# Gate, up and down of an expert: six transfers of 1 MB become three of 2 MB

## What is computed

```python
def one_block(args):
    tok, e, w = args
    xb = xt[tok]
    hb = jax.nn.silu(xb @ w_gate[e]) * (xb @ w_up[e])
    return (hb @ w_down[e]) * w[:, None].astype(h.dtype)
```

## Time and profile before

| | us |
|---|---|
| median of 3 runs | 1754.09 |
| lowest and highest | 1751.27, 1755.17 |
| the profiled execution | 1756.78 |
| its span, first to last instruction | 1754.9 |
| PE busy with matmuls | 1347.4 (77%) |
| DVE, ACT, POOL busy | 439.7, 177.8, 206.6 |
| moved by the transfer engines | 400.32 MB, 228 GB/s over the span |

### The profile page before, as it was taken

One profiled execution on the slowest core, in us unless ns is written; L12 is line 12 of the kernel. 1 busy time (PEld: TensorE's weight loads), 2 busy tenths in 40 slices (PEclk: granted clock), 3 DMA queues, 4 the chain that ended last, 5 costly groups with the idle time before them and its releaser, 6 DMA issues.

```text
span 1754.9 us, 27286 instructions
## 1 busy us (share of the span) xinstructions
PE 1347.4 (77%) x10122; PEld 690.7 (39%) x10123; DVE 439.7 (25%) x966; ACT 177.8 (10%) x464; POOL 206.6 (12%) x364
## 2 busy tenths in 40 slices
PE   7959987689667887787669999879437688887740
PEld 1124444432334444454312444655234344544420
DVE  0021126737301111111036001552640011111106
ACT  0000023300000000000001001441000000000000
POOL 0000000000011222222110000000001112222120
PEclk9979996789688898888779999598657778989875
DMA  9942330037199799899997542001029999598940
GB/s 344 357 152 96 115 101 1 1 119 252 51 395 396 287 385 401 330 377 400 404 365 235 130 125 87 22 1 48 24 74 398 406 406 391 196 399 314 361 140 36
DMA packets 102356, 400.32 MB, mean 228 GB/s; under 512 B 13765, under 2 KB 14053, under 8 KB 80809
## 3 DMA queue, kind: packets, MB, share of 16 engines
q1 hardware_dynamic: 79544, 341.88, 51.3%
q0 software_dynamic: 16848, 55.23, 9.4%
q10 hardware_dynamic: 5924, 2.71, 0.6%
HBM read 383.18 MB, written 16.74 MB: 228 GB/s over the span
## 4 chain that ended last, share of the span: by engine, by line
PE 46%; DMA 34%; DVE 8%; issue 4%; ACT 4%; DVEq 1%; POOL 1%; SPq 0%; POOLq 0%; ACTq 0%
DMA ring<-in_w_up_dram 20%; PE ps L694 19%; DMA xg<-xmod,idx 10%; PE ps L657 5%; PE ps L878 4%; PE ps L672 4%; PE ps L896 3%; PE ps L862 2%; PE ps L784 2%; ACT hT L575 2%; DMA mbias<-in_b_ada_dram 2%; PE ps L817 1%; DVE sums L1071 1%; DMA qkv<-ybuf 1%; PE ps L769 1%
## 5 line engine op out<-in xcount | busy, mean ns | idle before, releaser
L878 PE MATMUL ps<-ring,xs 128*32 128x256 f32 x4736 | 310.2, 417 | 91.6 <-DMA ring<-in_w_up_dram 78.7
L878 PEld LDWEIGHTS ps<-ring,xs 128*32 128x32 f32 x4736 | 172.2, 119 | 225.4 <-issue 143.1
L694 PE MATMUL ps<-ring,hT 128*128 128x512 f32 x576 | 250.3, 596 | 4.5 <-ACT hT L539 2.3
L896 PE MATMUL ps<-ring,hm 128*32 128x256 f32 x2368 | 190.2, 475 | 1.4 <-DMA ring<-in_w_down_dram 1.4
L694 PEld LDWEIGHTS ps<-ring,hT 128*128 128x128 f32 x576 | 109.8, 191 | 143.6 <-issue 136.9
L862 PE MATMUL ps<-cst,xg 32*128 32x32 f32 x608 | 93.5, 277 | 81.1 <-DMA xg<-xmod,idx 81.1
L862 PEld LDWEIGHTS ps<-cst,xg 32*128 32x128 f32 x608 | 77.5, 195 | 129.0 <-issue 121.7
L1300 DVE TENSOR_TENSOR hp<-sg,ps 128x128 f32<-128x128 f32 x74 | 21.3, 288 | 371.6 <-ACT sg L622 371.6
L896 PEld LDWEIGHTS ps<-ring,hm 128*32 128x32 f32 x2368 | 82.5, 132 | 68.4 <-issue 38.8
L672 PE MATMUL ps<-ring,cond 128*2 128x512 f32 x192 | 91.4, 633 | 4.1 <-issue 4.1
L657 PE MATMUL ps<-ring,cond 128*2 128x512 f32 x192 | 84.3, 602 | 10.3 <-ACT cond L520 10.3
(11 more groups left out here) (197 smaller groups left out, 964.9 us busy)
## 6 DMA issues: line engine op xcount, KB each, us to landing
ring<-in_w_gate_dram SPq DMA_DIRECT2D x82, 1024.0 KB, 14.7
ring<-in_w_up_dram SPq DMA_DIRECT2D x82, 1024.0 KB
ring<-in_w_down_dram SPq DMA_DIRECT2D x82, 1024.0 KB, 15.9
ring<-in_w_ada_dram SPq DMA_DIRECT2D x48, 1024.0 KB, 10.6
ring<-in_w_qkv_a_dram SPq DMA_DIRECT2D x12, 1024.0 KB, 4.9
ring<-in_w_qkv_b_dram SPq DMA_DIRECT2D x12, 1024.0 KB, 7.4
modb<-mdram POOLq DMA_DIRECT2D x16, 512.0 KB, 7.9
qkv<-ybuf POOLq DMA_DIRECT2D x2, 3072.0 KB, 18.8
```

The source lines that it names most:

```text
L694: ins = mm(ps[:, 2 * t + hf, :], lhs[:, k, t * P:(t + 1) * P], raw[:, slot, kk * D + hf * 512:kk * D + (hf + 1) * 512], start=(k == 0), st ...
L878: ins = mm(ps[j * BLK:(j + 1) * BLK, 1, 0:W].rearrange("p (a n) -> p a n", a=2), xs[:, k, :], w[:, :, at:at + FW], start=(k == 0), stop=(k ...
L896: ins = mm(ps[j * BLK:(j + 1) * BLK, 5, 0:WD], hm[:, 2 * c + q, :], ring[:, slot + GU + c, q * D + j * WD:q * D + (j + 1) * WD], start=(c ...
```

## The change

Each of the three matrices of an expert comes in one transfer of 2 MB. Gate now lies in slots 0 and 1, up in slots 2 and 3, down in slots 4 and 5; the halves k = 0 to 3 and 4 to 7 of a matrix are its two slots. `taken` names the second half of a block for every slot. `gate_up` waits once, for both matrices, and `down` once.

```diff
         def taken(l, s, start):
 
-            return (gu_used[l], start * 2 + (s // 2 + 1)) if s < GU else (dn_used[l], start * 2 + (s - GU + 1))
+            return (gu_used[l], start * 2 + 2) if s < GU else (dn_used[l], start * 2 + 2)
...
-                    for s in range(RING):
+                    for s in range(0, RING, 2):
                         if isinstance(i, int):
-                            sp.wait_ge(st_free, MOE0[l] + s + 1)
+                            sp.wait_ge(st_free, MOE0[l] + s + 2)
                         else:
 
                             sp.wait_ge(*taken(l, s, freed))
 
                             sp.wait_ge(moe_land[l][s], i * 16 + 16)
-                        dst = ring[:, bass.ds(base + s, 1), :]
+                        dst = ring[:, bass.ds(base + s, 2), :]
                         if s < GU:
-                            src = (w_gate, w_up)[s % 2][l, bass.ds(e, 1)]
-                            src = src.rearrange("a (p k) n -> p (a k) n", k=KD)[:, 4 * (s // 2):4 * (s // 2) + 4, :]
+                            src = (w_gate, w_up)[s // 2][l, bass.ds(e, 1)]
+                            src = src.rearrange("a (p k) n -> p (a k) n", k=KD)
                             dst = dst.rearrange("p a (k n) -> p (a k) n", k=4)
                         else:
-                            src = w_down[l, bass.ds(e, 1)]
-                            src = src.rearrange("a (c m p) n -> p (a c) m n", c=2, m=2)[:, s - GU, :, :]
+                            src = w_down[l, bass.ds(e, 1)].rearrange("a (m p) n -> p (a m) n", m=G)
                             dst = dst.rearrange("p a (m n) -> p (a m) n", m=2)
                         sp.dma_start(dst, src).then_inc(moe_land[l][s], 16)
...
                     pe.wait_ge(xs_rdy[l], b + 1)
                     for half in range(2):
-                        for s in (2 * half, 2 * half + 1):
-                            pe.wait_ge(moe_land[l][s], landed)
-                        w = ring[:, slot + 2 * half:slot + 2 * half + 2, :]
+                        if half == 0:
+                            pe.wait_ge(moe_land[l][0], landed)
+                            pe.wait_ge(moe_land[l][2], landed)
+                        w = ring[:, slot + half:slot + half + 3:2, :]
...
                     for c in range(2):
-                        pe.wait_ge(moe_land[l][GU + c], landed)
+                        if c == 0:
+                            pe.wait_ge(moe_land[l][GU], landed)
```

## The result

The change makes the kernel slower: 1791.7 us median (1787.11 to 1797.57, 4 runs) against 1753.05 us (1751.27 to 1755.17, 4 runs) of the kernel before in the same comparison, ratio 1.0222 with a 95% interval of 1.0182 to 1.0262. That is 38.7 us; 1781.9 was forecast, with a range of 1763 to 1795. The profiled execution took 1787.62 us with a span of 1785.7, 30.8 more than the one before; so the traces show 31 of the 38.7 us.

A forecast was written before the change was run, and what follows sets the result against it. The prediction took the weight stream to bound the full stretches and the blocks with their gathers those between; 2.0 + 6.7 + 11.2 - 4.1 + 12.0 = 27.8 us on 1754.1 gave 1781.9 us, range 1763 to 1795.

The forecast's parts named there:

- hand-overs: Where weight stream and PE pass work to each other: later refills (6.7 and 2.0 us) and later block starts (11.2 us).
- Refills: SP's refills wait for the second half of a pass: 6.7 us at four places, 2.0 at the start of layer 0.
- The four places: Where PE hands over to the stream, before 649, 779, 1327 and 1595 us; later refills there cost 6.7 us.
- Starts: PE waits for all 4 MB of gate and up before a block; five whole passes instead of second halves cost 11.2 us.
- Down: At layer 0's start both down transfers go together at 487.8 us, leaving a hole in the stream: 2.0 us.
- Longer runs: Gate and up write 16 KB per partition instead of 8; the stream rises from 426 to 434 GB/s: -4.1 us.
- Gathers: In stretches set by blocks, token-row gathers wait behind longer runs: 20 gathers at 0.6 us more, 12 us.
- the linear end: Upper value for a gather's added time from 8 to 16 KB runs, if linear in bytes: 0.86 us.
- the gathers don't mind: Rival: gathers unaffected by run length, only hand-overs and runs count: 15.8 us, 1769.9 us; chance 0.17.
- A new wait on top: Rival: later refills leave a multi-block expert behind a one-block expert short of weights: 37 us, 1791 us; chance 0.05.
- Larger transfers pay: Rival: fewer transfers save a fixed engine cost each; a third exposed gives 55 us back, 1727 us; chance 0.05.
- Hidden: Rival: other slack takes up the hand-overs and gathers don't change, so time stays at 1754 us; chance 0.03.

The follow-up runs named there:

- the kernel with runs of 8 KB: Changed kernel with gate in slots 0 and 2, up in 1 and 3, so 2 MB transfers write 8 KB runs: 1769.51 us, ratio 1.0099 to the kernel before.
- down alone: Kernel before, but an expert's down comes in one 2 MB transfer with one wait and one refill; gate and up as before: 1752.35 us, ratio 0.9995.

## Why the prediction was right, and where its sizes were off

The direction, the mechanism and the range held; the forecast was 10 us short. That the result lies in the range is in part luck: two terms were off in opposite directions. The hand-overs cost 16 to 17 us where 19.9 were forecast (6.7, 2.0 and 11.2), the length of the runs 21 to 23 where 7.9 were forecast. With the hand-overs as forecast, the time would have been 1794 to 1797 us, at the upper end of the range or over it. Step by step:

*Refills, 8.7 us.* Right in sum: 8.8 measured alone (4.4 to 13.3 by its interval). The four places and the start of the layer weren't measured apart.

*Starts, 11.2 us.* The mechanism is there: five passes of 24.08 us instead of 26.75, against 15.54 before, so 8.5 more. Its worth alone was 4.6 us, with an interval from 0 to 9.5. What I missed is that a lag of the blocks can come back in a stretch that they set, when later gathers fall behind the end of the transfers. That was seen in one such stretch, of this kernel and of the changed one. Together with the refills it came to 16.3, near the 19.9 of the prediction and a little more than the parts, within the intervals.

*Down.* The 2.0 us at the start of layer 0 couldn't be told from nothing. In the changed kernel SP issues down there at 487.86, as worked out (487.8), but the first hand-over comes only 0.5 us later than before (546.87 against 546.34).

*Longer runs, -4.1 us.* The rate went from 426 to between 426 and 434 GB/s where 434 was forecast, and experts in a full stretch became 0.15 us shorter instead of 0.18.

*Gathers, 12 us.* This term was mis-sized. I took 0.6 us for each of 20 gathers. In the three places shown they took 1.0, 1.3 and 1.6 us more than before, and by the medians 1.5 (7.8 against 6.3), which is above the linear end (0.86) of what two run lengths let expect. PE's wait for a gather rose from 1.7 us on the mean (81.1 over 47) to 3.1 (108.4 over 35). The term also took it that each block goes on waiting for its gather. Instead PE's own work behind a late gather, some of it at the lower clock, came onto the chain, for which I had no term. Against the kernel with runs of 8 KB, gate/up and down were busy 27.6 us more. Whole waits with runs of 8 KB or less had brought down's busy time from 190.2 us to 172.5 and 170.3, and the long runs took this back; I had neither. Together the length of the runs cost 21 to 23 us (the changed kernel against the one with runs of 8 KB), where longer runs and gathers together were to be 7.9.

*The rivals.* That the gathers don't mind is refuted by their own times, 8.0 us against 6.4 with runs of 8 KB in the same blocks. A new wait on top didn't come in the form described, short weights behind one-block experts; what came on top are longer gathers and the slow half blocks behind them. Larger transfers pay nothing that can be seen: down alone and the 2 MB transfers with old runs both show none of it, and their intervals, of 5 to 6 us to a side, leave no room for the 55 us of this rival. Hidden it was not.

The rule of the Trainium skill, page "DMA: Bandwidth & Descriptors", section "Queues, rings and completion order", that an engine takes turns between its queues packet by packet, agrees in direction with the gathers under runs of 4, 8 and 16 KB (medians 5.9, 6.3 and 7.8 us). The profile has each run as one packet (of 0.16, 0.31 and 0.61 us). That this is the packet of the rule, and that an engine changes queues only between two of them, is inferred from this order. The step from 8 to 16 KB (1.5 us) is over three times that from 4 to 8 (0.4), where a packet's time grows by 0.30 and 0.15 us, twice as much; why isn't settled. Nor was the price of the slow clock behind a gather measured apart from the gather's, and why whole waits with runs of 8 KB leave fewer slow halves than the kernel before has wasn't looked into.

## What to carry to other kernels

Where a stream of weights is already back to back with several transfers under way, joining transfers gives nothing; what moves is when consumers may start and buffers come free, and each hand-over between stream and engine pays half a tile's work. Look also at who else uses the transfer engines: a small gather on the critical cycle pays for the longest contiguous run of the stream beside it, so keep these runs short, here at 8 KB or less, even when the transfer is large (slots placed in turn do that). And look at what TensorE's matmuls cost behind such a gather: a half block at 1.2 GHz can come on top of the wait. The sum of an engine's busy time doesn't tell this; the chain does, by what moved onto it.

## What the runs showed of the hardware that was not expected

- A gather of 32 rows beside a stream of runs of 4 KB took 5.9 us (median; 5.7 to 8.2), of 8 KB 6.3 (6.1 to 7.0) and of 16 KB 7.8 (7.2 to 8.5), in the kernel with transfers of 2 MB and runs of 4 KB, in the kernel before and in the changed one. With no stream beside it it took 2.8 to 3.0 in the last two.
- The profile records each such run as one packet, which took 0.16, 0.31 and 0.61 us at 4, 8 and 16 KB (medians).
- After a pause of PE of 3.15 us the granted clock was 0.50 over the 6 us from 605 us on; after one of 1.51 us, with runs of 8 KB, it was 0.76 over the 7 us that hold it and what follows. Down took 3.64 and 3.12 us there, against 1.93 at the full clock. It isn't a rule for one pause: in the kernel before down behind 2.48 us took 1.93 and behind 1.51 us 3.62.
- The stream's rate hardly rises beyond runs of 8 KB: it was 386, 410, 426 and 426 to 434 GB/s at 2, 4, 8 and 16 KB.
